# Half of the merge of branches A and C, moved into the sparse attention of a hybrid mixer

## The reference, cut to what matters

```
ya = (head_rms(gla(...))   * silu(ga))    @ w_up_a     # branch A, 512 -> 1024
yb = dsa(...)                             @ w_up_b     # branch B, sparse attention, 512 -> 1024
yc = (head_rms(mlstm(...)) * sigmoid(oc)) @ w_up_c     # branch C, 512 -> 1024
g_a, g_b, g_c = split(sigmoid(h @ w_in[:, gates]), 3)  # 1024 -> 3 x 1024
x = x + g1 * ((g_a*ya + g_b*yb + g_c*yc) @ w_o)
```

## Time and profile before

| | |
|---|---|
| median of 3 runs | 1573.62 us (1572.13 to 1579.72) |
| the profiled execution | 1576.36 us, span 1574.6 us |
| PE busy | 1362.8 us, 87% of the span |
| DVE busy | 1073.2 us, 68% |
| ACT busy | 781.4 us, 50% |
| POOL busy | 405.1 us, 26% |
| from the end of branch C to the start of the merge | 385.5 to 572.2 us |
| the merge | 572.2 to 775.4 us |
| granted clock of PE, mean | 0.92 |

### The profile page before, as it was taken

The page is one execution under the profiler, slowest core; times in us unless marked ns, Lnnn a source line. Parts: engine busy times, 40 slices in busy tenths (PEclk is TensorE's granted clock), DMA queues, the critical chain, the costliest instruction groups (busy, mean ns, idle before and its releaser), DMA issues.

```text
span 1574.6 us, 19431 instructions
## 1 busy us (share of the span) xinstructions
PE 1362.8 (87%) x6418; PEld 1047.3 (67%) x6418; DVE 1073.2 (68%) x1312; ACT 781.4 (50%) x952; POOL 405.1 (26%) x295
## 2 busy tenths in 40 slices
PE   3899988986454889999897699999999999999984
PEld 1587868653122458888795378888888888888851
DVE  0437485376788836443445778888898898989827
ACT  3612232233122552222312178888888888888821
POOL 1100010000000000000000136666666666666610
PEclk9796989887766999999999899999999999999997
DMA  9133312102400033223413479999999999999955
GB/s 303 53 102 113 100 35 81 40 27 103 171 14 0 1 108 106 81 94 107 147 35 121 135 284 379 404 403 383 370 359 368 369 351 358 358 341 368 331 206 229
DMA packets 126009, 312.48 MB, mean 198 GB/s; under 512 B 24133, under 2 KB 61322, under 8 KB 117514
## 3 DMA queue, kind: packets, MB, share of 16 engines
q1 hardware_dynamic: 107674, 286.63, 50.5%
q0 software_dynamic: 18288, 25.21, 4.4%
HBM read 315.44 MB, written 37.75 MB: 224 GB/s over the span
## 4 chain that ended last, share of the span: by engine, by line
PE 57%; DVE 15%; DMA 13%; ACT 6%; issue 5%; POOL 2%; SPq 1%; POOLq 0%; DVEq 0%; ACTq 0%
PE bank L803 16%; PE bank L1146 8%; PE bank L808 8%; DMA arena<-h_dram,tok_of 6%; PE bank L1174 6%; DMA ring<-in_exp_w_up 4%; PE bank L1150 4%; PE bank L1133 2%; PE bank L871 2%; DVE arena L1852 2%; DVE top L1851 2%; POOL tok_of L702 1%; PE bank L1079 1%; ACT arena_parts L1480 1%; PE bank L1023 1%
## 5 line engine op out<-in xcount | busy, mean ns | idle before, releaser
L2088 DVE TENSOR_TENSOR ring_parts<-ring,arena_parts 128x2048 fp32r<-128x2048 f32 x186 | 423.1, 2289 | 61.1 <-ACT arena_parts L1480 60.6
L1480 ACT ACTIVATE arena_parts<-ring 128x2048 fp32r<-128x2048 f32 x186 | 355.9, 1930 | 49.4 <-DMA ring<-in_exp_w_up 45.3
L1146 PE MATMUL bank<-arena_parts,oTA_parts 128*128 128x512 f32 x496 | 200.0, 403 | 2.9 <-DVE oTC_parts L2103 1.5
L1146 PE MATMUL bank<-arena_parts,oTC_parts 128*128 128x512 f32 x496 | 194.7, 393 | 0.0
L1174 PE MATMUL bank<-arena_parts,oTB_parts 128*128 128x512 f32 x496 | 161.0, 406 | 5.2 <-DVE ring_parts L2088 5.1
L803 PE MATMUL bank<-hT_parts,ring_parts 128*128 128x512 f32 x344 | 145.7, 423 | 1.4 <-DVE arena L1708 1.4
L690 POOL DMA_INDIRECT arena<-h_dram,tok_of x63 | 128.6, 2042 | 56.3 <-POOL tok_of L702 52.7
L716 POOL DMA_INDIRECT y_dram<-arena,row_of x62 | 97.8, 1578 | 173.6 <-ACT arena L1507 170.8
L1257 ACT ACTIVATE ring_parts<-ring 128x2048 fp32r<-128x2048 f32 (+1 forms) x42 | 69.0, 1647 | 144.3 <-DMA ring<-in_w_in 85.6
L803 PE MATMUL bank<-x_parts,ring_parts 128*128 128x512 f32 x344 | 138.6, 403 | 0.0
L1150 PE MATMUL bank<-ring_parts,oTA_parts 128*128 128x512 f32 x496 | 134.2, 393 | 0.0
(11 more groups left out here) (403 smaller groups left out, 2346.8 us busy)
## 6 DMA issues: line engine op xcount, KB each, us to landing
ring<-in_exp_w_gate SPq DMA_DIRECT2D x124, 512.0 KB, 5.4
ring<-in_exp_w_up SPq DMA_DIRECT2D x124, 512.0 KB, 9.5
ring<-in_exp_w_down SPq DMA_DIRECT2D x62, 1024.0 KB, 9.6
ring<-in_w_in SPq DMA_DIRECT2D x25, 1024.0 KB, 5.3
ring<-in_ada_w SPq DMA_DIRECT2D x16, 1024.0 KB, 5.2
arena<-y_dram SPq DMA_DIRECT2D x8, 1536.0 KB, 9.5
arena<-in_ada_w SPq DMA_DIRECT2D x4, 2048.0 KB, 13.3
x<-in_x SPq DMA_DIRECT2D x2, 2048.0 KB, 8.8
```

The lines of the kernel that those rows point to most:

```text
L1146: mm(out_gu, t[c][:, tile_cols(4 * k + j)], hi[:, :, j, :], start=(k == 0 and j == 0 and x_ == 0), stop=False)
L1480: A(w_hi[c][k], w_raw[c][k], ACT.Copy).then_inc(sem("gu_hi_ready" if k < 2 else "down_hi_ready"), 1)
L2088: v.tensor_tensor(w_lo[c][k], w_raw[c][k], w_hi[c][k].bitcast(F32), ALU.subtract).then_inc(sem("gu_lo_ready" if k < 2 else "down_lo_ready" ...
```

## The change

Four of the twelve merge steps, those of branches A and C for m = 0 and 2 (columns 0 to 511), run inside the sparse attention. Their gates are still split products on PE, with the high part made on ACT and the low part on POOL in four pieces of 512 columns. Their up products are plain fp32 matmuls on the unsplit tiles. ACT takes the sigmoid and copies the up product out of PSUM, and POOL multiplies and adds. The sum goes to DRAM (`m_dram`) and comes back into `mT` before the merge, which has 8 steps left and begins with branch B. To make room, `pb3` to `pb7` and `mb3` to `mb7` move into the attention loop, n = 0 to 5, and DVE's split of `wg0` and `wu0` moves from n = 4 to n = 5.

```diff
+def early_steps():
+    return [(m, b) for m in (0, 2) for b in (0, 2)]
 def merge_steps():
-    return [(m, b) for m in range(0, 8, 2) for b in range(3)]
+    return [(m, 1) for m in (0, 2)] + [(m, b) for m in (4, 6) for b in range(3)]
+SPLIT_ORDER = (1, 0, 2)
...
+        L = [qiT[:, b, :] for b in range(2)]
+        rbE = Region(arena, 19328, END)
+        sgateE, upE, accE = rbE.take(2, T), rbE.take(2, T), rbE.take(2, T)
+        m_dram = nc.dram_tensor("m_dram", [2, P, 2 * T], F32).ap()
+        for n, (m, b) in enumerate(early_steps()):
+            load_cols(f"wgE{n}", COL["gates"] + D * b + P * m, f"eg{n}1")
+            load(f"wuE{n}", [(0, (4, 256), ups[b][:, :, P * m:P * m + 256])], f"eu{n}1", split=False)
         for c in range(3, 8):
             load_cond(c)
-        cond = [*condA, *condC, qlT[:, 0, :], qlT[:, 1, :]]
+        cond = [*condA, *[cn[:, c % 2, :] for c in range(3, 8)]]
# SP
+                if name in ("wuE3", "adr41"):
+                    q = 0 if name == "wuE3" else 1
+                    sp.wait_ge(sem("eprod_ready"), 4 * q + 4)
+                    sp.dma_start(m_dram[q], accE.rearrange("p a b -> p (a b)")).then_inc(sem("early_moved"), 16)
                 if name == "wg1":
                     sp.wait_ge(sem("oTB_ready"), 4)
+                    sp.wait_ge(sem("early_moved"), 32)
+                    for q in range(2):
+                        sp.dma_start(mT[:, 2 * q:2 * q + 2, :].rearrange("p a b -> p (a b)"), m_dram[q]
+                                     ).then_inc(sem("early_moved"), 16)
# POOL
+            def split_lo(name):
+                pool.wait_ge(sem("lo_split"), splits.index(name))
+                split_wait(pool, name, "hi_split")
+                out_, raw_, hi_ = lo_view(name, 1, 2048), ring_view(name, 0, 1, 2048), hi_view(name, 1, 2048).bitcast(F32)
+                for q in range(4):
+                    c_ = slice(512 * q, 512 * q + 512)
+                    ins = g.tensor_tensor(out_[:, :, c_], raw_[:, :, c_], hi_[:, :, c_], ALU.subtract)
...
+            split_lo("wgE0")
             pool.wait_ge(sem("oTC_ready"), 4)
...
+            for n in range(4):
+                if n < 3:
+                    split_lo(f"wgE{n + 1}")
+                early_products(n)
# PE
             mean_square(3)
-            further_condition(3)
+            def early_gates(n):
+                for r in range(2):
+                    project(f"eg{n}{r}", f"wgE{n}", r)
+            def early_ups(n):
+                br = early_steps()[n][1]
+                loaded(pe, f"wuE{n}")
+                w = ring_view(f"wuE{n}", 0, 4, 256)
...
+                for r in range(2):
+                    b = begin(f"eu{n}{r}")
+                    for j in range(4):
+                        ins = mm(b[:, :], w[:, j, tile_cols(r)], oT[br][:, j, :], start=(j == 0), stop=(j == 3))
+                    end(ins)
+            early_gates(0)
...
-            further_condition(4)
+            early_ups(0)
             pe.wait_ge(sem("wi0_ready"), 1)
...
                 for h in range(8):
+                    if i > 1 and h == 2:
+                        early_gates(i - 1)
+                        early_ups(i - 1)
...
-                further_condition(4 + i)
...
-            for c in range(3, 8):
-                column_sums(f"mb{c}", 4 + c, cond[c])
...
+            early_gates(3)
+            early_ups(3)
             npt = 0
             for n in range(-1, 8):
...
+                if n in range(5):
+                    further_condition(n + 3)
+                if n in range(1, 6):
+                    column_sums(f"mb{n + 2}", n + 6, cond[n + 2])
                 if n < 0:
                     continue
# ACT
+                if h == 2:
+                    split_hi("wgE0")
...
                 for h in range(8):
+                    if i > 1 and h == 2:
+                        early_sigmoids(i - 1)
+                        split_hi(f"wgE{i}")
+                        early_copies(i - 1)
# DVE
-                if i == TT - 1:
-                    for c in range(3, 8):
-                        further_columns(c)
...
+                    if n == 1:
+                        dve.wait_ge(sem("eprod_ready"), 8)
...
+                if n in range(1, 6):
+                    further_columns(n + 2)
```

More of the change, by code:

```diff
@@ L83, in product_order, with early @@
         out += [(f"num{h}", "hC_ready", h + 1), (f"den{h}", "den_read", h + 1)]
-    out += [("msC3", "root_ready", 8), ("pb3", "cond_ready", 8)]
-    out += [("msq", "root_ready", 9), ("mskv", "root_ready", 10), ("pb4", "cond_ready", 9)]
+    out += [("msC3", "root_ready", 8)]
+    def early(n, kind):
+        return [(f"{kind}{n}{r}", {"eg": "esig_ready", "eu": "eup_ready"}[kind], 2 * n + r + 1) for r in range(2)]
+    out += early(0, "eg")
+    out += [("msq", "root_ready", 9), ("mskv", "root_ready", 10)]
+    out += early(0, "eu")
     out += [("wi", "wcol_ready", 1), ("uk", "ukT_ready", 1)]
@@ L90, in product_order @@
     for i in range(1, 4):
-        out += [(f"ix{i}{h}", "relu_ready", 8 * (i - 1) + h + 1) for h in range(8)]
-        out += [(f"pb{4 + i}", "cond_ready", 9 + i)]
+        for h in range(8):
+            out += early(i - 1, "eg") + early(i - 1, "eu") if i > 1 and h == 2 else []
+            out += [(f"ix{i}{h}", "relu_ready", 8 * (i - 1) + h + 1)]
     out += [(f"q{m}", "q_ready", m + 1) for m in range(4)]
-    out += [(f"mb{c}", "mb_ready", c + 1) for c in range(3, 8)]
     out += [(f"ql{h}", "ql_ready", h + 1) for h in range(8)]
+    out += early(3, "eg") + early(3, "eu")
     for n in range(-1, 8):
@@ L100, in product_order @@
             out += [(f"lg{i}{h}", "L_ready", 8 * i + h + 1) for h in range(4 * g, 4 * g + 4)]
+        out += [(f"pb{n + 3}", "cond_ready", n + 8)] if n in range(5) else []
+        out += [(f"mb{n + 2}", "mb_ready", n + 3)] if n in range(1, 6) else []
         if n >= 0:
@@ L249, in hybrid_kernel @@
         hD = rc.take(T)
-        condC = [rc.take(T) for _ in range(3)]
         rb = Region(arena, 0, END)
@@ L268, in hybrid_kernel @@
         Pn, PT, olT = rb2.take(8, T), rb2.take(TT, T), rb2.take(8, T)
-        L = [rb2.take(T) for _ in range(2)]
+        L = [qiT[:, b, :] for b in range(2)]
+        rbE = Region(arena, 19328, END)
+        sgateE, upE, accE = rbE.take(2, T), rbE.take(2, T), rbE.take(2, T)
         nmax, psum = sb("nmax", [P, 8]), sb("psum", [P, 8])
@@ L1386, in _, with early_sigmoids, early_copies @@
             act.wait_ge(sem("oTC_ready"), 4)
-            keep_condition("pb3", cond[3])
+            def early_sigmoids(n):
+                for r in range(2):
+                    b = done(act, f"eg{n}{r}")
+                    if n:
+                        act.wait_ge(sem("eprod_ready"), 2 * n + r - 1)
+                    A(sgateE[:, r, :], b[:, :], ACT.Sigmoid).then_inc(sem("esig_ready"), 1)
+            def early_copies(n):
+                for r in range(2):
+                    b = done(act, f"eu{n}{r}")
+                    A(upE[:, r, :], b[:, :], ACT.Copy).then_inc(sem("eup_ready"), 1)
             for n in range(3):
@@ L1393, in _ @@
                 A(rsB[:, n, :], b[:, :], ACT.Sqrt, scale=1.0 / (256, 128)[n], bias=epsc[:, 0:1]).then_inc(sem("root_ready"), 1)
-            keep_condition("pb4", cond[4])
+            early_sigmoids(0)
+            split_hi("wgE1")
+            early_copies(0)
             b = done(act, "ckr")
@@ L1451, in _ @@
                 split_hi(names[1])
[L1452 removed]
+                if br == 2 or m < 4:
                     for r in range(2):
@@ L1919, in _ @@
                     if br:
+                        if m < 4:
+                            dve.wait_ge(sem("early_moved"), 64)
                         ins = v.tensor_tensor(mT[:, m + r, :], mT[:, m + r, :], mtmp[r], ALU.add)
-                        if br == 1:
+                        if br == 1 and m >= 4:
                             link(ins)
```

47 lines of the change are left out of this document (35 added, 12 removed).

## The result

The changed kernel takes 1520.84 us (median of 4 runs, 1517.87 to 1524.25), the kernel before 1572.88 us in the same job (4 runs, 1565.73 to 1579.72): a ratio of 0.9683, 95% interval 0.9655 to 0.9711. The forecast was 1520. The profiled execution took 1524.25 us.

What follows compares the result with a forecast made beforehand. Merge bound by PE alone, selection by a serial DVE chain with PE idle beside it. -65.2 + 7.0 - 7.9 + 0.5 + 11 + 1 = -53.6 us takes the median of 1573.62 to 1520 us; range 1505 to 1540.

Steps and rivals of the forecast that it cites:

- four merge steps gone: Merge: four steps of 16.3 us without an `mr` go, 72 matmuls by 0.227 us each, -65.2 us.
- step 0, less `pb3` and `pb4`: Ahead of the selection: gates and ups delay `wi` and DVE's reciprocal by 7.0 us, bounds 5 to 15.
- wait for `mb`: Selection, block 3: the `mb` sums no longer stand ahead of its rounds, so DVE's wait goes, -7.9 us.
- table load on ACT: End of the selection: ACT's table load for the exponentials no longer has time in hand, +0.5 us.
- POOL beside DVE: Selection and loop: the sum held no term for DVE slowed by POOL; POOL's own 1.2 us pieces counted as hidden.
- `pb` and `mb` in the loop: Attention loop: the moved products lengthen PE's path, 2.8 us each for n = 1 to 4; +11 us, bounds 5 to 18.
- `wg1` late: Start of the merge: two 512 KB loads now stand ahead of `wg1`, plus 1 us, at most 5.
- steps 1 to 3: Beside the selection: early steps hidden, cost 0; to spare some 2 us for the first, 7 the second, 2.6 the third.
- Rival (b): Selection: PE stays at the low clock as every idle gap brings it back, 33 us more, 1553 us; chance 0.08.
- Rival (d): Attention loop: moved products hidden where PE waits for DVE, plus 3 instead of 11; 1510 us, down to 1500; chance 0.1.
- Rival (c): Selection and loop: POOL slows DVE to two thirds while it works, 17 us longer, 1537 us; chance 0.13.
- MAX8 over 0.69 us: Sign on DVE that POOL slows it or that POOL's pieces become a serial bound; POOL's 512 columns over 3 us likewise.

Runs made afterwards that it cites:

- `wg1` first: Against the changed kernel, SP loads `wg1` ahead of the wait for branch B and the early sum's loads; 1516.14 us beside 1518.86 in one job.

## Why the prediction was right

Term by term, forecast and aligned traces:

| term | forecast | measured |
|---|---|---|
| four merge steps gone | -65.2 | -65.3 |
| wait ahead of `wo` | 0 | -0.5 |
| step 0, less `pb3` and `pb4` | +7.0 | +6.6, 6.9 at block 1 |
| wait for `mb` | -7.9 | -7.8 |
| table load on ACT | +0.5 | 0.0 |
| POOL beside DVE | 0 | +3.7 |
| `pb` and `mb` in the loop | +11 | +9.8 |
| `wg1` late | +1 | +1.75 |
| steps 1 to 3 | 0 | 0 |

The -65.3 is what is left of the measured -64.1 without the 1.75 and the -0.5; 4 by 72 by 0.227 is 65.4.

- *What bounded the kernel* was read rightly. The merge was PE alone, so a step taken out of it was worth its own length. The selection was DVE alone, so three steps of 18 us lay beside it and cost nothing as PE's work; the run with steps 1 to 3 short, read beside the one where POOL waits, shows it. The margins were not as small as forecast. For step 3, 2.6 us: PE starts the first logits at 497.58, and DVE takes them at 502.15, 4.6 us later. For step 1, 2 us: ACT waits 4.30 us for DVE ahead of the third head's relu, and 1.56 us where POOL is held back.
- *The clock.* In the changed kernel the matmuls of `eg0` start 0.43 us apart until 381.60, and 0.23 apart from 381.92. The forecast had 383 in the time of before. From 400 to 500 us the granted clock is 0.86 to 1.00 in the windows after, and 1.00 beside the last rounds instead of 0.64. Rival (b) falls. Its "every idle gap brings it back" does not hold: in the kernel before, the granted clock is 1.00 from 548 to 572 us, with PE idle for 3.19 us in it.
- *The loop* was the least certain term, 5 to 18. Its composition was not quite as said. The iteration with n = 1 takes 3.4 us more, those with n = 2, 3 and 4 1.5, 2.2 and 1.7 instead of 2.8 each, as part of a `pb` and `mb` fills gaps. The iterations from n = 5 on take 1.75 instead of 0.9, and the higher clock at the start gives 0.7 instead of 2. The transfers cost nothing. Without the early steps, the moves cost 8.2 us, 1.6 less, although one `pb` there waits 0.44 us for its load. The traces show where: the iterations n = 2 to 5 take the same in both (7.84, 8.81, 9.88 and 9.13 us), and 0.5 us lie ahead of n = 1, 0.6 in it and 0.6 behind n = 5. The low clock is in each of these places: in the changed kernel the granted clock is 0.50 from 508.1 to 511.5, and the logits at 509.07 take 3.10 us against 1.89 (from 553 to 583 it is 0.83 against 0.89). It is not the early steps as such, since the loop is 79.6 us long with step 0 short and with step 0 moved, too, and 79.5 with none. What places these stretches stays open. Rival (d), 3 us, falls.
- *POOL* was right as to its own work (1.25 us for 512 columns against 1.2) and wrong as to DVE: the sum had nothing for it. Rival (c) named the mechanism and overpriced it, 17 us against 3.7, because the rounds, most of the selection, are MAX8 and MATCH_REPLACE8, which keep their durations, and most of POOL's work lies beside them. The sentence that gave MAX8 over 0.69 us as the sign to look for named an instruction that could not show it: in the kernel before, too, it took up to 695 ns. The two misses (+3.7 here, -1.2 in the loop) and the small ones add up to the 2.1 us between -53.6 and -51.5.
- *Luck.* The mechanism was right but for POOL beside DVE, and the sum was 2.1 us too hopeful. That the median, 1520.84 us, stands within 1 us of the forecast 1520 is luck: the sizes that were off, 3.7 us at POOL and 1.2 in the loop, lie on opposite sides, the head, which no term was about, was 1.5 us shorter in the changed kernel's profile, and POOL's products of step 3 just missed the last mask, which would have cost 1.7 us more.

The Trainium skill bears on this in two places. Its GPSIMD Engine Reference, Key points, says that POOL contends with DVE instructions that have two SBUF inputs; SBUF — State Buffer, Who interferes with whom, says that whichever engine issues first has the shared ports for its whole instruction and the other blocks, and that an instruction with one SBUF input does not contend outside of certain modes. The trace agrees for SCALAR_TENSOR_TENSOR and COPY_PREDICATED, and for MAX8. It agrees that they take turns (1634 ns against 1593). It does not agree that nothing overlaps: alone the two would add up to 0.75 + 1.25 = 2.0 us a pair, and a pair takes 1.67. TENSOR_SCALAR, with one tile and a column of scalars, was slowed too (0.41 to 1.42 us). The profile does not name the mode it ran in, but its durations alone fit one of those certain modes: 128 columns more cost it 0.06 us (0.35, 0.41 and 0.48 us for 256, 384 and 512), half of the 0.13 that they cost SCALAR_TENSOR_TENSOR (0.62 and 0.75 us for 384 and 512).

## What to carry to other kernels

- A stage where one engine is full and a stage where it idles beside another engine's serial chain are worth looking for as a pair. Work moved from the first to the second gained its whole length there and cost nothing here, up to the moment where the chain waits for it. Compute that margin for each piece (1.6 us was the least here, with POOL held back; 7.2 us of further products ahead made the third head 1.33 us late), and keep the pieces away from the products ahead of the chain's start, where they count in full (step 0 cost 7 us there, and a later place gave 4.9 us of it back at the first logits).
- Before putting elementwise work on POOL, look at which DVE instructions will be beside it, not at how much DVE does in the stage. Hold POOL back with one semaphore over those that it slows, and let it run beside the others. Then look at every later place where the two can now meet: here the first hold won 3.7 us and the last mask lost 1.7 of them again.
- Where executions differ by more than the effect looked for, align the traces at the last point that the edit cannot touch, follow them to a point behind everything that it can touch, and put kernels that are to be compared into one job.

## What the runs showed of the hardware that I had not expected

- DVE and POOL take turns, instruction by instruction: 1634 ns for one of 752 beside POOL's of 1593. Both lose: POOL's 1.25 us became 1.59.
- MAX8 and MATCH_REPLACE8 keep their durations beside POOL (MATCH_REPLACE8 0.41 us for 256 columns, MAX8 0.56 for 384, with POOL busy and without). So does DVE's reciprocal, 3.35 us with POOL busy beside it and without.
- The copy `wi` on DVE and POOL's `IOTA`, which reads nothing, slowed each other as well: the copy took 1.14 us where `IOTA` started first and 0.41 where the copy did, and `IOTA` 0.89 and 1.17.
- The time to the end of branch C differs by up to 7 us between profiled executions of kernels whose code there is all but the same (378.4 to 385.6 us). Between the changed kernel and `wg1` first, whose code is the same up to there, the 5.6 us have all arisen by 166 us. What makes it so stays open.
